# Paged attention of a decoder step: keys turned by VectorE in 32x32 blocks, scores on quarter rows

## The chip, the cores and the metric

The kernel runs on one core of a Trainium2 chip. The metric is the device time of one launch in microseconds (us); the median of several runs counts. One further execution was profiled, and all rows below come from it.

## The reference, cut to what matters

The program is one step of a two-layer decoder for a prompt of 512 tokens and for 8 samples of 8 new tokens each. All of it is float32. The second layer's attention has 8 heads over a shared latent of 512 channels and a rotary key of 64:

```python
def latent_scores(q_lat, q_rope, c, kr):
    s = jnp.einsum('bqhc,bkc->bhqk', q_lat, c, ...)
    s = s + jnp.einsum('bqhr,bkr->bhqk', q_rope, kr, ...)
    return s * SM_SCALE
...
    past_c = cache_kv_latent[page_table].reshape(DB, past_len, KV_LORA)
    past_kr = cache_k_rope[page_table].reshape(DB, past_len, QK_ROPE)
```

Each sample has its own 2048 past keys, in 16 pages of 128 keys that `page_table` names, and its 8 new ones; softmax runs over both, and the probabilities are multiplied with the same latents. For one sample there are 8 heads x 8 tokens = 64 query rows. The pages are 16 x (256 + 32) KB for a sample and 37.7 MB for all eight. The change touches this attention of the samples and the last head of the prompt's attention before it. The convolution, the MLPs and all projections stay.

## The kernel before

Everything is scheduled by hand with semaphores, and each engine works its own list in order. SP (SyncE) issues nearly all loads. PE (TensorE) runs the dense products, about 9,600 matmuls of 128x128 by 288 columns in three parts of float32r (L2422 to L2424). Their weights land in `RAW`, a ring of 4 slabs, and ScalarE (L733) and GpSimd (L1416, L1418) split them into high and low parts `WH` and `WL`.

The prompt's attention goes head by head (L2948 on). For each of four blocks of queries there are scores (`head_scores`, L2908 and L2909, counted by `s_mm`), mask and top on VectorE, the exponential on ScalarE, and the turn of the probabilities (`head_turn`, L2918). Once a head comes its output (`head_out`, L2928, counted by `pv_mm`) and the samples' latent queries (`head_uk`, `head_latent`, kept in `QLAT`). In the last head PE also puts the samples' rotary queries in order (`sample_ropes`, L2936, `QRS`).

The samples' attention follows, as `sequence(i, ...)` for eight samples; 1 to 6 are a loop (`Fori`). A slab is four pages in one place of `RAW`. For each slab j of sample i PE does this, in this order (L3072 to L3087):

- `scores(j, i)`: 5 steps of 128 channels (the last for the rotary part), each for two halves of the slab on separate column tiles: 64 query rows to PSUM partitions 0 to 63 and 64 to 127 of bank 2 (L3025);
- `keys(...)` of the next slab: 16 + 2 transposes of 128x128 (L2983, L2988) into PSUM, which ScalarE (L1323) and VectorE (L2294, L2308) copy to `KEYS` and `ROPES`;
- `values(j - 1, i)`: probabilities times latents, 4 matmuls of 512 columns (L3059), each of them two instructions, as every float32 matmul is;
- `turn(j, i)`: the two transposes of the probabilities (L3035), after VectorE's top (L2315) and ScalarE's exponential (L1340).

Once a sample come the new keys (`new_keys`, L3013 and L3014), the exchange between the two halves (`swap`, L3043) and the output (`give`, L3068). VectorE rescales and adds up the outputs (L2339, L2342). Behind the last slab PE goes on with the output projections (`product("wo", ...)`, and `w_uv` at L3111).

On SP, `cache_loads` is a loop over samples:

```python
            with sp.Fori(0, NS) as i:
                sp.dma_start(table[:], io["page_table"][bass.ds(i, 1), :]).then_inc(table_in, 16)
...
                for j in range(RING):
                    pages = [sp.value_load(table[0:1, 4 * j + q:4 * j + q + 1], min_val=0,
...
                    sp.wait_ge(pe_read_raw, 1 + j + RING * i)
...
                    for q in range(4):
```

In its innermost body there is one DMA for a page's latents (L464, 128 rows of 2 KB) and one for its rotary keys (L468, 128 rows of 256 B). The wait says that PE has read the slab that lay there. A `value_load` (L456) reads one page number into a register. `dense("wo", ...)` (L496) and the two slabs of `w_uv` (L618) are issued behind `cache_loads`.

## Time and profile before

| | us |
|---|---|
| median of 3 runs (1822.06 to 1822.7) | 1822.65 |
| the profiled execution, its own time | 1821.97 |
| its span, in which the rows are counted | 1820.2 |
| PE busy | 1735.6 (95%) |
| VectorE busy | 914.2 (50%) |
| ScalarE busy | 739.2 (41%) |
| GpSimd busy | 966.6 (53%) |
| DMA, mean over the span | 109 GB/s |

A row of a group gives the line, the engine, the operation, the output and inputs with their shapes, the count, the busy time in us and the mean of one in ns, and then the engine's idle time before it with what ended it. Busy time counts stretches in which instructions overlap once, so that 640 matmuls of 384 ns can be busy for 76 us. Register, semaphore and DMA-issuing instructions are not counted as busy; the latter are seen on the timeline of their queue (SPq, ACTq). PEclk is the share of full speed (2.4 GHz) that was granted.

### The profile page before, as it was taken

Reading aid. Unit: us, or ns where it says so; the run is one execution under the profiler, and the core shown is the slowest. Engines: PE = TensorE matmul, PEld = TensorE weight load, DVE = VectorE, ACT = ScalarE, POOL = GpSimd, SP = SyncE. Lnnn points to the kernel's source line nnn. Section 1 sums busy time; section 2 is a strip of 40 time slices with the busy share of each in tenths; the row PEclk is TensorE's granted clock in tenths of the full one; section 3 lists DMA queues with packets and bytes.
Section 4 is the critical chain, followed back from the end, with each engine's and each line's share of the span. In section 5 each row is a group of like instructions: output and inputs, shape, how many; then the busy total and the mean of one; then the engine's idle time right before and its main releaser. Section 6 shows DMA issues by size and latency. Waiting matters only on the chain. (4 is left out here: it accounts for less than half of the span.)

```text
span 1820.2 us, 33590 instructions
## 1 busy us (share of the span) xinstructions
PE 1735.6 (95%) x12402; PEld 1578.6 (87%) x12402; DVE 914.2 (50%) x2228; ACT 739.2 (41%) x1463; POOL 966.6 (53%) x795
## 2 busy tenths in 40 slices
PE   7998899999999999899899899999989999999998
PEld 6997799998899999898776566666989999999988
DVE  5897799943423636673455444444261222222283
ACT  5565444454444543632233333333343222232342
POOL 4994799977799984753210000002655445554652
PEclk9998999999999999999999999999999999999999
DMA  7321455544355540323002155556412222322201
GB/s 205 106 87 56 121 180 163 163 152 139 117 162 162 164 148 26 120 66 117 13 0 79 52 157 156 156 155 207 139 63 77 70 92 92 92 69 69 93 24 53
DMA packets 183947, 198.58 MB, mean 109 GB/s; under 512 B 33065, under 2 KB 138115, under 8 KB 183826
## 3 DMA queue, kind: packets, MB, share of 16 engines
q1 hardware_dynamic: 179726, 194.28, 34.8%
q10 hardware_dynamic: 4100, 2.68, 0.5%
q8 instruction: 76, 1.25, 0.3%
q14 instruction: 45, 0.37, 0.1%
HBM read 192.14 MB, written 4.79 MB: 108 GB/s over the span
## 5 line engine op out<-in xcount | busy, mean ns | idle before, releaser
L1418 POOL TENSOR_TENSOR WL<-RAW,WH 128x1024 fp32r<-128x1024 f32 (+3 forms) x279 | 574.4, 2067 | 256.1 <-ACT WH L733 254.5
L2422 PE MATMUL bank<-AH,WH 128*128 128x288 f32 x2080 | 626.3, 301 | 30.6 <-DVE AL L1672 13.9
L2423 PE MATMUL bank<-AL,WH 128*128 128x288 f32 x2080 | 617.0, 297 | 0.0
L2424 PE MATMUL bank<-AH,WL 128*128 128x288 f32 x2080 | 616.7, 297 | 0.0
L2422 PEld LDWEIGHTS bank<-AH,WH 128*128 128x128 f32 x2080 | 394.6, 190 | 42.2 <-DVE AL L1672 16.7
L733 ACT ACTIVATE WH<-RAW 128x1024 fp32r<-128x1024 f32 (+1 forms) x281 | 292.0, 1045 | 264.9 <-PE bank L2424 264.4
L2423 PEld LDWEIGHTS bank<-AL,WH 128*128 128x128 f32 x2080 | 394.8, 190 | 0.7
L2424 PEld LDWEIGHTS bank<-AH,WL 128*128 128x128 f32 x2080 | 394.5, 190 | 0.0
L2422 PE MATMUL bank<-BH,WH 128*128 128x288 f32 (+1 forms) x1120 | 336.9, 301 | 13.7 <-DVE S L1721 4.1
L1416 POOL TENSOR_TENSOR WL<-RAW,WH 128x256 fp32r<-128x256 f32 (+2 forms) x135 | 119.2, 903 | 416.4 <-ACT WH L733 416.4
L2424 PE MATMUL bank<-BH,WL 128*128 128x288 f32 (+1 forms) x1120 | 333.4, 298 | 0.0
L2423 PE MATMUL bank<-BL,WH 128*128 128x288 f32 (+1 forms) x1120 | 333.3, 298 | 0.0
L2422 PEld LDWEIGHTS bank<-BH,WH 128*128 128x128 f32 x1120 | 210.5, 188 | 19.1 <-issue 15.2
L2424 PEld LDWEIGHTS bank<-BH,WL 128*128 128x128 f32 x1120 | 210.6, 188 | 1.4
L2423 PEld LDWEIGHTS bank<-BL,WH 128*128 128x128 f32 x1120 | 210.6, 188 | 1.3
L1797 DVE SCALAR_TENSOR_TENSOR bank<-S,taps,bank 128x224 f32<-128x224 f32 x464 | 134.7, 365 | 0.0
L1998 DVE TENSOR_TENSOR prod<-R,bank 128x288 f32<-128x288 f32 x64 | 29.0, 454 | 176.3 <-ACT R L1083 100.5
L2007 DVE TENSOR_TENSOR Y<-Y,bank 128x288 f32<-128x288 f32 x112 | 50.7, 453 | 110.9 <-PE bank L2424 110.9
L1443 POOL TENSOR_TENSOR acc<-acc,sq 128x288 f32<-128x288 f32 x97 | 78.5, 815 | 31.6 <-ACT sq L751 26.9
L1591 POOL TENSOR_TENSOR BL<-prod,BH 128x288 fp32r<-128x288 f32 x64 | 51.3, 806 | 67.1 <-ACT BH L1087 67.1
L3025 PE MATMUL bank<-Y,prod 128*64 128x256 f32 x640 | 76.1, 384 | 0.5 <-ACT Y L1323 0.4
L1885 DVE TENSOR_TENSOR Y<-Y,bank 128x288 f32<-128x288 f32 x112 | 49.7, 448 | 49.0 <-PE bank L2424 49.0
(298 smaller groups left out, 2131.6 us busy)
## 6 DMA issues: line engine op xcount, KB each, us to landing
RAW<-in_w_up SPq DMA_DIRECT2D x48, 1024.0 KB, 5.5
RAW<-in_w_down SPq DMA_DIRECT2D x48, 1024.0 KB, 5.1
RAW<-in_cache_kv_latent SPq DMA_DIRECT2D x128, 256.0 KB, 2.9
RAW<-in_conv_pw SPq DMA_DIRECT2D x16, 512.0 KB, 7.3
RAW<-in_conv_pw SPq DMA_DIRECT2D x8, 1024.0 KB, 5.2
RAW<-in_ple_gate SPq DMA_DIRECT2D x8, 1024.0 KB, 5.1
RAW<-in_cache_k_rope SPq DMA_DIRECT2D x128, 32.0 KB, 2.9
RAW<-in_w_o SPq DMA_DIRECT2D x4, 1024.0 KB, 6.1
```

Source lines behind the costliest of these rows:

```text
L733: nc.scalar.activation(split_part(WH, d, q), raw_part(d, q), ACT.Copy).then_inc(hi_done, 1)
L1416: nc.gpsimd.tensor_tensor(dst[:, 0:a], src[:, 0:a], hi[:, 0:a], ALU.subtract)
L1418: nc.gpsimd.tensor_tensor(dst, src, hi, ALU.subtract).then_inc(lo_done, 1)
L1443: nc.gpsimd.tensor_tensor(dst, dst, src, ALU.add).then_inc(acc_done, 1)
L1591: nc.gpsimd.tensor_tensor(half(BL, m, h), prod[:, n % 2, :], half(BH, m, h).bitcast(F32), ALU.subtract).then_inc(u_lo, 1)
L1797: nc.vector.scalar_tensor_tensor(out=run if c < CW - 1 else out, in0=src, scalar=w, in1=run, op0=ALU.mult, op1=ALU.add).then_inc(conv_late, 1)
L1885: nc.vector.tensor_tensor(half(Y, m, h), half(Y, m, h), bank[u % BANKS][:, 0:H], ALU.add)\
L2007: nc.vector.tensor_tensor(half(Y, m, h), half(Y, m, h), bank[u % BANKS][:, 0:H], ALU.add)\
L2422: nc.tensor.matmul(out, wh, xh, start=first, stop=False)
L2423: nc.tensor.matmul(out, wh, xl, start=False, stop=False)
L2424: return nc.tensor.matmul(out, wl, xh, start=False, stop=last)
L3025: ins = nc.tensor.matmul(bank[2][64 * g:64 * g + 64, 0:256], q, k, start=c == 0, stop=c == 4)
```

## The change

A unit is now eight pages (1024 keys), two for a sample, 16 in all; all loops over units on PE, ScalarE and VectorE are written out.

- PE no longer transposes pages. VectorE turns them in 32x32 blocks, from SBUF to SBUF: `turn_pages` 4 pages with 2048 elements a partition in one instruction, `turn_ropes` 256. A page's turned keys lie together in `TURN` (576 columns a page: 18 blocks of 32 channels), so that the write is one run and a matmul reads four runs of 32, one from each of four pages.
- After such a turn the four quarters of the partitions hold different keys, and each has 32 channels at a time. `scores(u)` is 18 blocks x 4 quarters x 2 column halves = 144 matmuls, of 32 rows, 64 columns and 128 moving columns. The quarters write to four banks, the halves to two sets of partitions.
- The queries must lie in each of the quarters. `queries(i)` does that with 18 DMAs of 256 B rows from SBUF to SBUF, issued by ScalarE: for sample 0 ahead of the last exponential of head 7, for the others behind the even units.
- The units lie in `RAW` (two slabs) and in `WIDE`, a place over `WH` and `WL`, in turn. Unit u takes the place of u - 4 and waits for `unit_read`, which `values` counts. The high parts of `wo` wait for 14 units read, the low parts for 15.
- The new keys of all samples are multiplied at once and masked (`KZ`, `NMASK`), with no gather and no transposes for each sample.
- On SP, samples 0 and 1 are issued in pieces, each piece when its room is free, and samples 2 to 7 in a loop of two samples. A number, a latent DMA and a rotary DMA for each page stay.

The core of the diff:

```diff
-        bank = [ctx.enter_context(nc.psum_tensor(f"bank{i}", [P, 512], F32)) for i in range(8)]
+        PS = ctx.enter_context(nc.psum_tensor("bank", [P, 8, 512], F32))
+        bank = [PS[:, i, :] for i in range(8)]
...
-        QRS = S[:, 5184:5696]
+        QRS = [S[:, 5184:5696], R1[:, :, :].rearrange("p a b -> p (a b)")[:, 0:TP]]
+        Q4 = [S[:, 1152 * e:1152 * e + 1152].rearrange("p (b q) -> p b q", b=18) for e in range(2)]
...
+        TURN = [TURNED, yflat.rearrange("p (k c) -> p k c", k=8)]
...
+            pages_of(slice(0, 1))
+            sp.wait_ge(ones_set, 1)
+            sp.wait_ge(lo_done, PART0[DENSE0["kvh"] + 4])
+            sp.wait_ge(pe_read_raw, 2)
+            for s in range(2):
+                pages = [page(4 * s + q) for q in range(4)]
+                load_latents(0, s, pages)
+                load_ropes(0, s, pages)
+            sp.wait_ge(kvt_done, NH)
+            sp.wait_ge(v_mm, NH // 2)
+            for s in range(2):
+                load_latents(1, s, [page(8 + 4 * s + q) for q in range(4)])
+            sp.wait_ge(s_mm, 4 * NH)
+            for s in range(2):
+                load_ropes(1, s, [page(8 + 4 * s + q) for q in range(4)])
+            pages_of(slice(1, 2))
+            for s in range(2):
+                load_latents(2, s, [page(4 * s + q) for q in range(4)])
+            sp.wait_ge(pe_read_raw, 4)
+            sp.wait_ge(pv_mm, NH)
+            for s in range(2):
+                load_ropes(2, s, [page(4 * s + q) for q in range(4)])
+            for s in range(2):
+                pages = [page(8 + 4 * s + q) for q in range(4)]
+                load_latents(3, s, pages)
+                load_ropes(3, s, pages)
+            with sp.Fori(1, NS // 2) as i:
+                for e in range(2):
+                    pages_of(bass.ds(2 * i + e, 1))
+                    for k in (2 * e, 2 * e + 1):
+                        pages = [page(8 * (k % 2) + q) for q in range(8)]
+                        sp.wait_ge(unit_read, 4 * i + k - 3)
+                        sp.wait_ge(ones_set, 1)
+                        for s in range(2):
+                            load_latents(k, s, pages[4 * s:4 * s + 4])
+                            load_ropes(k, s, pages[4 * s:4 * s + 4])
...
+            def queries(i):
+                for m in range(4):
+                    for a in range(4):
+                        act.dma_start(Q4[i % 2][32 * a:32 * a + 32, 0:16].rearrange("p (c m) q -> p m c q", m=4)[:, m],
+                                      QLAT[32 * m:32 * m + 32, :, 64 * i:64 * i + 64]).then_inc(q4_in, 16)
+                for r in range(2):
+                    act.dma_start(Q4[i % 2][:, 16 + r], QRS[r][:, 64 * i:64 * i + 64]).then_inc(q4_in, 16)
...
+                else:
+                    act.wait_ge(ql_used, NH)
+                    act.wait_ge(qrs_c, 2)
+                    queries(0)
...
+            def turn_pages(u, s):
+                dve.wait_ge(*half_landed(u, s))
+                if u >= 2:
+                    dve.wait_ge(score_mm, u - 1)
+                nc.vector.transpose(TURN[u % 2][:, 4 * s:4 * s + 4, 0:CL],
+                                    half_pages(u, s).rearrange("p (k c) -> p k c", k=4)).then_inc(keys_turned, 1)
+            def turn_ropes(u, s):
+                dve.wait_ge(*half_landed(u, s))
+                nc.vector.transpose(TURN[u % 2][:, 4 * s:4 * s + 4, CL:CL + DR],
+                                    half_ropes(u, s).rearrange("p (k c) -> p k c", k=4)).then_inc(keys_turned, 1)
...
+            for u in range(1, UNITS2):
+                i, j = divmod(u, 2)
+                if u < UNITS2 - 1:
+                    turn_pages(u + 1, 0)
+                    turn_pages(u + 1, 1)
+                unit_top(u)
+                if u < UNITS2 - 1:
+                    turn_ropes(u + 1, 0)
+                    turn_ropes(u + 1, 1)
+                unit_sum(u)
+                if j and i:
+                    keep(i - 1)
+                if j:
+                    gain_output(u - 1)
+                else:
+                    finish(i - 1)
+                if j and i < NS - 1:
+                    new_top(i + 1)
...
+            def new_keys(i):
+                pe.wait_ge(q4_in, 16 * Q4_LOADS * (i + 1))
+                if i > 1:
+                    pe.wait_ge(swap_read, i - 1)
+                dst = new_score_bank(i)
+                for c in range(4):
+                    nc.tensor.matmul(dst, QLAT[:, c, 64 * i:64 * i + 64], CS[:, c, :], start=c == 0, stop=False)
+                for r in range(2):
+                    ins = nc.tensor.matmul(dst, Q4[i % 2][:, 16 + r, :], KZ[:, r, :], start=False, stop=r == 1)
+                ins.then_inc(new_mm, 1)
+            def scores(u):
+                pe.wait_ge(keys_turned, CHUNKS * (u + 1))
+                for b in range(18):
+                    for a in range(4):
+                        rows32 = slice(32 * a, 32 * a + 32)
+                        for g in range(2):
+                            ins = nc.tensor.matmul(score_bank(u, a)[64 * g:64 * g + 64], Q4[u // 2 % 2][rows32, b, :],
+                                                   TURN[u % 2][rows32, 4 * g:4 * g + 4, 32 * b:32 * b + 32], start=b == 0, stop=b == 17)
+                ins.then_inc(score_mm, 1)
+            def turn(u):
+                i, j = divmod(u, 2)
+                pe.wait_ge(exp_done, 2 * u + (1 if j else 2))
+                if j == 0 and i > 1:
+                    pe.wait_ge(lat_out, i - 1)
+                for k in range(4):
+                    ins = nc.tensor.transpose(bank[1][:, k * P:(k + 1) * P], SP[:, k * P:(k + 1) * P], ident[:, :])
+                if j == 0:
+                    ins = nc.tensor.transpose(bank[3][0:64, 0:64], PN, ident[0:64, 0:64])
+                ins.then_inc(spt_mm, 1)
...
+            hd = NH - 1
+            head_scores(hd, 0)
+            head_uk(hd)
+            head_turn(hd - 1, 3)
+            head_scores(hd, 1)
+            head_out(hd - 1)
+            head_latent(hd)
+            sample_ropes()
+            head_turn(hd, 0)
+            head_scores(hd, 2)
+            head_turn(hd, 1)
+            head_scores(hd, 3)
+            head_turn(hd, 2)
+            pe.wait_ge(ql_used, NH)
+            pe.wait_ge(qrs_c, 2)
+            new_keys(0)
+            scores(0)
+            head_turn(hd, 3)
+            head_out(hd)
+            pe.wait_ge(pt_used, 4 * NH)
+            for c in range(4):
+                ins = nc.tensor.transpose(bank[6][0:TS, c * P:(c + 1) * P], CS[:, c, :], ident[:, :])
+            ins.then_inc(csn_mm, 1)
+            turn(0)
+            for u in range(1, UNITS2):
+                i, j = divmod(u, 2)
+                if u == 1:
+                    pe.wait_ge(csn_set, 1)
+                    pe.wait_ge(a_lo, A("o", 0, NH - 1))
+                scores(u)
+                if j and i:
+                    give(i - 1)
+                values(u - 1)
+                turn(u)
+                if j and i < NS - 1:
                     new_keys(i + 1)
-            keys(0, 0, range(3))
-            pe.wait_ge(a_lo, A("o", 0, NH - 1))
-            pe.wait_ge(ql_used, NH)
-            keys(0, 0, (3, 4))
-            new_keys(0)
-            sequence(0, True, False)
-            with pe.Fori(1, NS - 1) as i:
-                sequence(i, False, False)
-            sequence(NS - 1, False, True)
-            values(3, NS - 1)
+            values(UNITS2 - 1)
             product("wo", None, 0, 1)
             give(NS - 1)
-            pe.wait_ge(swap_read, NS)
...
```

`values(u)` and `give(i)` do the same matmuls as before, in other places; `unit_top(u)` is one reduction over four banks and two small instructions for eight pages, where `slab` had that for four. `set_constants` takes the place of `set_dup` in head 1, with some eight small instructions more; `sample_ropes` does its eight matmuls twice.

## Rows read from the trace of the kernel before

**Rows 1.** The page, section 4: the chain that ended last, shares of the span.
```profile
PE bank L2422 9%; PE bank L2424 9%; PE bank L2423 9%; PE bank L3025 4%; PE bank L3059 3%; PE bank L2983 3%; PE bank L3035 1%; DVE bank L1700 0%; PE bank L3068 0%; PE bank L3052 0%; PE bank L2988 0%; DVE X L1710 0%; POOL WL L1416 0%; PE bank L3136 0%; PE bank L3013 0%
```

**Rows 2.** 1060 to 1260 us: length; PE, PEld, DVE, ACT, POOL busy; PEclk; DMA share; GB/s.
```profile
1060.00:1260.00 200.00, 200.00 (x1453) 121.00 (x1451) 94.09 (x258) 72.56 (x212) 1.10 (x1) 1.00 0.53 156
```

**Rows 3.** Groups of PE instructions: total busy us, mean ns | idle before.
```profile
L3025 PE MATMUL bank<-Y,prod 128*64 128x256 f32 x640 | 76.1, 384 | 0.5 <-ACT Y L1323 0.4
L2983 PE MATMUL bank<-ident,RAW 128*128 128x128 f32 x512 | 63.0, 277 | 0.0
L3059 PE MATMUL bank<-RAW,S 128*64 128x512 f32 x256 | 61.9, 604 | 0.0
...
L3035 PE MATMUL bank<-ident,scaled 128*128 128x128 f32 x64 | 13.9, 299 | 0.0
L2988 PE MATMUL bank<-ident,RAW 128*128 128x128 f32 x64 | 12.2, 273 | 0.0
```

**Rows 4.** Timeline of PE: start us, duration us, instructions; new keys, last values.
```profile
1054.00 0.63 PE L3013 MATMUL bank<-acc,prod 128*64 128x8 f32 x8
...
1234.04 0.63 PE L3013 MATMUL bank<-acc,prod 128*64 128x8 f32 x8
...
1262.85 1.94 PE L3059 MATMUL bank<-RAW,S 128*64 128x512 f32 x8
```

**Rows 5.** SP's page loads by line: duration ns min/median/max; landing of the latents.
```profile
L464 SPq DMA_DIRECT2D RAW<-in_cache_kv_latent x128: 332/333/360, 969.7 to 1245.0; - x128
...
DMA to landing us min/median/max: 2.4/2.9/3.2
L468 SPq DMA_DIRECT2D RAW<-in_cache_k_rope x128: 332/333/933, 970.3 to 1245.5; - x128
```

**Rows 6.** Timeline of SP: start us, duration us, the DMA issued.
```profile
1155.51 0.33 SPq L468 DMA_DIRECT2D RAW<-in_cache_k_rope  x1
...
1160.90 0.34 SPq L464 DMA_DIRECT2D RAW<-in_cache_kv_latent  x1
...
1164.54 0.33 SPq L468 DMA_DIRECT2D RAW<-in_cache_k_rope  x1
1167.54 0.33 SPq L464 DMA_DIRECT2D RAW<-in_cache_kv_latent  x1
...
1245.53 0.33 SPq L468 DMA_DIRECT2D RAW<-in_cache_k_rope  x1
...
1261.52 3.68 SPq L618 DMA_DIRECT2D RAW<-in_w_uv  x2
```

**Rows 7.** Waits of SP's queue, 900 to 1300 us: total, times, longest.
```profile
SPq L464 <- PE bank L3059: 27.2, 10, 17.9
```

**Rows 8.** Timeline of PE: L3111, two column tiles, all pairs.
```profile
1272.13 3.71 PE L3111 MATMUL bank<-RAW,Y 128*64 128x128 f32 x64
```

**Rows 9.** Groups of VectorE, 1060 to 1260 us: total busy us, mean ns.
```profile
L2342 DVE SCALAR_TENSOR_TENSOR S<-S,acc,bank 128x512 f32<-128x512 f32 x20 | 15.0, 748 | 21.1 <-PE bank L3059 21.1
...
L2283 DVE COPY prod<-S 128x256 f32 x6 | 1.7, 278 | 0.0
```

**Rows 10.** Timeline of PE in the last head: idle before in brackets.
```profile
1008.50 0.33 PE L2918 MATMUL bank<-ident,prod 128*128 128x128 f32 x1 [2.16 <-DVE prod L2231]
...
1013.22 1.02 PE L2909 MATMUL bank<-S 128*128 128x512 f32 x2
```

**Rows 11.** Head outputs on PE's timeline; 1017 to 1023 with the columns of rows 2.
```profile
1003.91 2.42 PE L2928 MATMUL bank<-S,root 128*128 128x512 f32 x8 [0.17 <-ACT S L1287]
...
1018.72 4.63 PE L2928 MATMUL bank<-S,root 128*128 128x512 f32 x8 [0.69 <-ACT S L1287]
...
1017.00:1023.00 6.00, 5.24 (x12) 3.02 (x13) 0.36 (x2) 0.60 (x1) 0.00 (x0) 0.52 0.33 101
```

**Rows 12.** SP's issue of 2 KB rows, beside ScalarE's (L549) and alone (L631).
```profile
L549 SPq DMA_DIRECT2D Y<-in_x_prompt x8: 400/432/615, 0.8 to 4.9; - x8
L631 SPq DMA_DIRECT2D out_y_prompt<-Y x8: 332/356/567, 1805.4 to 1817.1; - x8
```

More of the change, by code:

```diff
@@ L274, in decoder_step @@
             pass
+        with nc.sbuf_tensor("TURNED", [P, 8, 18 * 32], F32) as TURNED:
+            pass
         BH, BL = sb("BH", [P, FC, T], F32R), sb("BL", [P, FC, T], F32R)
@@ new lines, in page, with load_latents @@
+            def page(n):
+                return sp.value_load(table[0:1, n:n + 1], min_val=0, max_val=io["cache_kv_latent"].shape[0] - 1)
+            def load_latents(u, s, pages):
+                dst = half_pages(u, s).rearrange("p (a c) -> p a c", a=1)
+                for q in range(4):
+                    sp.dma_start(dst[:, :, q * CL:(q + 1) * CL],
+                                 io["cache_kv_latent"].rearrange("n p c -> p n c")[:, bass.ds(pages[q], 1)])\
+                        .then_inc(half_landed(u, s)[0], 16)
@@ L2253, in _ @@
+            for hd in range(NH - 1):
                 top(hd, 0)
@@ L2367, in sequence @@
-            def sequence(i, first, last):
-                for j in range(4):
-                    slab(j, i, first, last and j == 3)
-                    if j:
-                        gain_output(j - 1, i)
-                    elif not first:
-                        finish(i - 1)
-                if not last:
-                    new_top(i + 1)
-            nc.vector.memset(QSR, 0.0).then_inc(qsr_zero, 1)
-            nc.vector.memset(NKR[DR:P], 0.0).then_inc(qsr_zero, 1)
-            nc.vector.memset(col(TOP, 4), NEG).then_inc(qsr_zero, 1)
@@ L2940, in _, with give @@
+            def give(i):
+                pe.wait_ge(out_done, OUTS + OUTS * i)
+                if i < NS - 1:
+                    pe.wait_ge(spt_c, 3 * (i + 1) + 2)
+                for c in range(4):
+                    ins = nc.tensor.matmul(give_bank(i)[:, c * 64:(c + 1) * 64], OUT[:, c * P:(c + 1) * P], JOIN,
+                                           start=True, stop=True)
+                ins.then_inc(out_mm, 1)
             rot(1, QR[:, 0, :])
@@ L2947, in _ @@
             pe.wait_ge(kv_staged, 10)
-            for hd in range(NH):
-                more, pair = hd < NH - 1, hd % 2 == 1 and hd < NH - 1
+            for hd in range(NH - 1):
+                pair = hd % 2 == 1
                 head_scores(hd, 0)
@@ L2960, in _ @@
                 head_uk(hd)
-                if not more:
-                    sample_ropes()
                 head_turn(hd, 1)
@@ L3063, in give @@
-            def give(i):
-                pe.wait_ge(out_done, OUTS + OUTS * i)
-                pe.sem_inc(seen, 1)
-                for c in range(4):
-                    ins = nc.tensor.matmul(bank[7][:, c * 64:(c + 1) * 64], OUT[:, c * P:(c + 1) * P], JOIN, start=True,
-                                           stop=True)
-                ins.then_inc(out_mm, 1)
-            def sequence(i, first, last):
-                for j in range(4):
-                    scores(j, i)
-                    if j == 1 and not first:
-                        give(i - 1)
-                    if not (last and j == 3):
-                        keys(*((j + 1, i) if j < 3 else (0, i + 1)), range(5))
-                    if j:
-                        values(j - 1, i)
-                    elif not first:
-                        values(3, i - 1)
-                    turn(j, i)
-                if not last:
-                    new_keys(i + 1)
@@ new lines, in _ @@
+            head_out(hd - 1)
+            head_latent(hd)
+            sample_ropes()
+            head_turn(hd, 0)
[8 more added lines that the diff above has]
+            head_turn(hd, 3)
+            head_out(hd)
+            pe.wait_ge(pt_used, 4 * NH)
+            for c in range(4):
+                ins = nc.tensor.transpose(bank[6][0:TS, c * P:(c + 1) * P], CS[:, c, :], ident[:, :])
```

522 lines of the change are left out of this document (243 added, 279 removed).

## The prediction

> **What bounds the kernel now.** The page's chain that ended last is PE all through, and after the dense products it names three lines of the paged attention: L3025 (scores), L3059 (values) and L2983 (page transposes) [rows 1]. The change touches that stage and the last attention head before it, so I asked for the stage alone: from 1060 to 1260 us PE is busy without a gap, VectorE 94 of 200 us, ScalarE 73, the DMA engines 53% at 156 GB/s [rows 2]. The groups of PE say what it does there: scores 76.1 us, page transposes 63.0 + 12.2, values 61.9, transposes of weights 13.9 [rows 3]. One sample (four slabs of four pages) takes (1234.04 - 1054.00) / 6 = 30.0 us of PE [rows 4]. PE bounds the stage.
>
> Next I asked what comes right behind PE. The page doesn't show it, because DMA-issuing and register instructions are not counted as busy; the timeline of SP, which issues every page load, does. Its DMAs start 0.52 us apart (7 spacings from 1160.90 to 1164.54), and from the last of a slab to the first of the next there are 3.0 us: a spacing, 0.2 for waits, and four page numbers read, 0.55 to 0.57 each [rows 5, 6]. So a sample costs SP 32 x 0.517 = 16.5, 16 x 0.55 = 8.8, the page table with the loop's end 2.5 (the 5.4 us from 1155.51 to 1160.90, less a spacing, four numbers and a wait), four waits 0.8: **28.6 us of SP, against 30.0 of PE**. The waits agree: SP waited 27.2 us for L3059, 17.9 of it at once, so 9.3 / 6 = 1.5 us a sample [rows 7]. SP is 5% away from being the bound.
>
> **What the change takes off PE.** All page transposes, 75.2 us. The scores become 144 matmuls a unit (8 pages), of 32 rows, 64 columns and 128 moving columns. No matmul on quarter rows is in the trace. The nearest is L3111, two column tiles side by side with 128 moving columns: 64 instructions, which are 16 pairs in two passes, in 3.71 us, 0.232 us a pair [rows 8]. If all eight tiles run side by side, a unit's scores cost 18 x 0.232 = 4.2 us; if the four row groups follow one another, four times that, 16.7. I take 4.2: the pair shows that separate tiles overlap, and the row groups write to four different banks. Values and weight transposes keep their work. A sample is then 30.0 - 75.2/8 - 76.1/8 + 2 x 4.2 = 19.5, with the wider new-key matmuls about 20: **10 us of PE a unit, against 15.0**.
>
> The Trainium skill ("TensorEngine Tiling (Array Packing)", Instruction Overhead) has a rule against many small matmuls: each has an overhead of about 60 cycles, however small. By it the 288 instructions of a unit take 7.2 us (an estimate, at 2.4 GHz), and the last scores would end 3 us later than in the sum below. No trace here has such matmuls yet.
>
> **What it adds, and what hides it.** VectorE turns 2048 elements twice a unit and 256 twice. No 32x32 turn is in the trace; the nearest, an SBUF copy of 128x256, took 278 ns, 1.07 ns an element, so 2.2 and 0.3 us (lower end); as an upper end I take four times that, since no row limits it; I take the lower, as passes here go by their elements. With a top over 512 (at most 0.75), its scale, the sum, the gain of 0.75 and half a finish and a keep, a unit costs VectorE 5.1 + 3.4 = 8.5 us [rows 9]. ScalarE loses its key copies and gets 18 DMAs a sample, 6 to 11 us at 0.35 to 0.6 each. The DMA engines get 2304 packets of 256 B a sample more, at 53% now [rows 2]. All of this lies under SP's pace, below; without that cover the units would go at PE's 10.
>
> **What it leaves.** SP's work for a page: one number, one latent DMA, one rope DMA. Only two of four waits and every second loop end go: 28.6 - 0.5 = **28.1 us a sample, 14.05 a unit**. So PE hands the bound to SP, and 8 of the 10 us a sample that PE gains become waiting for `keys_turned`. SP itself waits for no buffer: unit u takes the place of u - 4, which was read about 15 us before.
>
> **The sum**, along SP's queue. It goes on at the prompt's last scores (`s_mm` 32), in the trace at 1013.22 + 1.02 = 1014.2 [rows 10]. Head 7 gets a turn of pages ahead of its first mask (2.2) and a doubled `sample_ropes` (1.9, where PE now waits 2.2, so mostly covered): with the constants of head 1, +3.0, so 1017.2. Then ropes of unit 1 (8 numbers, 8 DMAs: 8.5), the table 2.2, latents of unit 2 (8.5), its ropes (8.5), unit 3 (12.7): 40.4. The wait for `pv_mm` among them comes at 1036.4; the last head's output stands behind queries(0) and scores(0) on PE and should be there at about 1034: nothing, with 2 us to spare. Six samples: 168.6. **SP's last issue is done at 1226.2**; before, it is at 1245.9 [rows 6].
> The tail: landed 2.9 after its start [rows 5], 1228.6; the second half turned 2.2, the top of unit 14, which stands between, 0.9, ropes 0.7: 1232.4; scores 4.2, give 1.1, values(14) 3.8 (two slabs of 1.94, overlapping [rows 4]), turn and copy 1.3, swap and values(15) 4.1: 1246.9.
> PE now idles some 4 us in each unit. Where it waited just before the stage, the granted clock was 0.52 for 6 us, that is mostly at 1.2 GHz, and eight matmuls took 4.63 us that took 2.42 before [rows 11]. Earlier units absorb such a loss; I add 2.2 once, at the end: 1249.1.
> ScalarE issues DMAs at the same time as SP. Where both issued, in the kernel's first 6 us, SP's DMAs of 2 KB rows took 432 ns (median), alone at the end 356 [rows 12]: 0.08 more. Of the 126 from queries(1) on, two thirds meet one of SP's: 0 to 8 us on the queue. I take 4: 1253.1. Before, the last values end at 1264.8 [rows 4]. Gain 11.7.
> Behind it, both slabs of w_uv come free only with values(15), where before the first came free 3.3 us ahead of the second; they were issued at 1261.5 and 1264.8 and used at 1272.1 [rows 6, 8]. About 1.5 us of that shows now. The low parts of wo, held until values(14), need 2 us and have 5: nothing. **Net -10.2 us**: 1821.97 - 10.2 = 1811.8 against the profiled execution's own time (its span is 1820.2, 1.8 less); the median of the runs shown, 1822.65, is 0.7 above it, so **1812**. (Cross-check: 6 x (30.0 - 28.1) = 11.4 in the loop.) About 0.2%, 3.6 us, is what a measurement of this kernel can tell from no change.
>
> **Rivals.**
> A, the forecast: SP's issue is the bound, 1801 to 1818. Chance 0.62.
> B, no change that shows: A, with the ScalarE DMAs at their upper end (+4), scores near 7 us (+3), and `pv_mm` late, since 18 DMAs stand ahead of exp(7,3) on ScalarE (+2): about 1821. 0.13.
> C, slower: issue is one path for both queues, and each of the 126 DMAs holds SP for its own 0.333 us, 42 us in the place of my 4: 1850. It decides from 0.11 us a DMA on (14 us, A's gain and 4). For it: 432 against 356. Against it: that is a quarter of the price. In part or whole 0.09.
> D, slower: an engine's new work is dear. With row groups in series PE needs 16.7 + 5.8 = 22.5 a unit; sixteen from about 1026 end at 1026 + 360 + 4 = 1390, 125 us later: 1947. PE overtakes SP from scores of 14.05 - 5.8 = 8.2 us a unit. Turns at four times the copy's rate give VectorE 5.1 x 4 + 3.4 = 23.8, about the same end. For it: nothing here shows either operation. Against it: the pair's overlap, and passes that go by elements. 0.11.
> E, all of PE's gain shows: 16 x 10 from 1026, and 4, end at 1190: 1748. SP's spacing would have to shrink; of 256 DMAs the shortest took 332 ns and the median 333 [rows 5]. 0.05.
>
> **How the numbers follow.** Faster: A and E, 0.67. Same: B, 0.13. Slower: C and D, 0.20. The range: below, A without contention (4), the clock's 2.2, head 7's 3 and w_uv's 1.5, 1812 - 11 = 1801, leaving out E; above, B and the smaller half of C, to 1835, leaving out D and the rest of C.
>
> **What would show it.** SP's DMAs in the loop 0.52 us apart, 56 us from one pair of samples to the next, and no wait for `unit_read`. PE idle about 4 us a unit ahead of the scores, released by VectorE's turns, and those by DMA landings. Scores 4 us a unit, turns 2.2 us each. The last values ending near 1253. It is wrong if SP waits for PE (then PE or VectorE bounds), if SP's spacing grows while ScalarE issues, or if page loads are issued sooner than 28 us a sample.

## The result, and the profile after

The kernel after takes **1836.53 us** (median of 5 runs, 1833.14 to 1842.3), the kernel before 1822.7 beside it (1822.06 to 1823.71): ratio 1.0075, 95% interval 1.0053 to 1.0097, slower by 13.8 us. The profiled execution of after is itself at 1836.53, its span 1834.7. The forecast of 1812.0 was wrong in sign, and the range (to 1835.0) missed by 1.5 us.

The page of after: busy time by engine, the granted clock in 40 slices, two DMA queues, and the chain that ended last ([rows 1]).

```profile
PE 1694.4 (92%) x15798; PEld 1562.1 (85%) x15798; DVE 930.7 (51%) x2134; ACT 682.3 (37%) x1296; POOL 967.1 (53%) x795
PEclk9998999999999999999999888889999999999999
q1 hardware_dynamic: 179726, 194.28, 34.0%
q8 instruction: 111, 1.82, 0.4%
PE 65%; DVE 9%; POOL 9%; SPq 7%; issue 5%; ACT 3%; DMA 1%; ACTq 1%; POOLq 0%; DVEq 0%
```

SP's queue (7%) is on the chain now. The same stretch as [rows 2]: PE is busy for 159 of 200 us, at a granted clock of 0.85.

```profile
1060.00:1260.00 200.00, 159.39 (x4132) 102.00 (x4118) 101.82 (x167) 23.07 (x70) 0.00 (x0) 0.85 0.62 179
```

PE's groups from 1026 to 1275 us, all 16 units: busy, mean ns, idle before and what ended it ([rows 3]).

```profile
L3089 PE MATMUL bank<-TURNED,S 32*64 32x128 f32 x2304 | 42.8, 297 | 18.8 <-issue 18.8
L3089 PE MATMUL bank<-Y,S 32*64 32x128 f32 x2304 | 41.9, 289 | 22.4 <-issue 18.2 <-DVE Y L2378 4.2
```

The scores are 84.7 us for 16 units, 5.3 each (4.2 forecast, at full clock), so the row groups do run side by side. But 37.0 us of idle time lies inside them, marked "issue": PE waited for no semaphore. I call such a stretch a hole. The timeline of PE shows them in the middle of a unit's 288 matmul instructions:

```profile
1093.47 3.09 PE L3089 MATMUL bank<-TURNED,S 32*64 32x128 f32 x199
1097.73 1.59 PE L3089 MATMUL bank<-TURNED,S 32*64 32x128 f32 x89 [1.16 <-issue]
1099.24 0.38 PE L3111 MATMUL bank<-S,scaled 128*128 128x2 f32 x2
1099.56 3.65 PE L3127 MATMUL bank<-RAW,root 128*64 128x512 f32 x16
...
1103.90 4.07 PE L3089 MATMUL bank<-Y,S 32*64 32x128 f32 x270
1109.76 0.59 PE L3089 MATMUL bank<-Y,S 32*64 32x128 f32 x18 [1.79 <-issue]
```

Queue 8 of the page carries packets of 16 KB with instructions. From 1060 to 1250 us there are 30 of them for 4,007 matmul and 3,993 weight-load records, 267 a packet, so I take a packet for 256 instructions (an estimate). One is in flight from 1095.34 to 1096.47; the hole ends 1.26 us later. All 19 holes end so, 1.0 to 1.6 us behind the end of a packet. A unit's scores are 144 weight loads and matmuls of two passes, 576 instructions, more than two packets.

Two more groups, over the same 16 units, tell how near PE itself is to the bound: the turn of the probabilities (L3100, its idle time and what ended it behind the bar) and half of the values.

```profile
L3100 PE MATMUL bank<-ident,prod 128*128 128x128 f32 x64 | 10.8, 294 | 7.1 <-ACT prod L1437 4.8 <-ACT S L1441 2.2
L3127 PE MATMUL bank<-WIDE,root 128*64 128x512 f32 x128 | 40.9, 725 | 0.0
```

PE waited for turned keys once (4.2 us, at unit 1) and for exponentials 7.1 us in all. The rest of its time is work and holes: it is as near the bound as SP. The DMA view from 1060 to 1250 us, before and then after:

```profile
q8 instruction: 3, 0.05, 0.1%
```
```profile
q8 instruction: 30, 0.49, 1.1%
```

SP's page loads ([rows 5]): a third of a microsecond as a rule, but some take six times that. Its waits from 1000 to 1280 us ([rows 7]) have none for `unit_read`, as forecast, and one for `pv_mm` (L539) that the sum had at nothing.

```profile
L508 SPq DMA_DIRECT2D RAW<-in_cache_kv_latent x64: 332/333/2022, 971.4 to 1244.6; - x64
...
L508 SPq DMA_DIRECT2D WIDE<-in_cache_kv_latent x64: 332/333/1664, 996.5 to 1230.3; - x64
```
```profile
SPq L498 <- DMA table<-in_page_table: 8.8, 7, 1.8
SPq L539 <- PE bank L3056: 4.2, 1, 4.2
```

SP's timeline ([rows 6]): the end of the prologue (all page loads ahead of the loop of six samples), four stretched groups, the last page load. A sample takes (1247.0 - 1064.55) / 6 = 30.4 us, where 28.1 was forecast.

```profile
1064.55 0.29 SPq L496 DMA_DIRECT2D table<-in_page_table  x1
...
1100.91 1.89 SPq L508 DMA_DIRECT2D WIDE<-in_cache_kv_latent  x4
1102.98 3.19 SPq L516 DMA_DIRECT2D S<-in_cache_k_rope  x4
1106.36 3.38 SPq L508 DMA_DIRECT2D WIDE<-in_cache_kv_latent  x4
1109.92 2.35 SPq L516 DMA_DIRECT2D S<-in_cache_k_rope  x4
...
1245.16 1.88 SPq L516 DMA_DIRECT2D RAW<-in_cache_k_rope  x4
```

SP's records of these six samples add up to 182.5 us, which are 167.3 of its own work and 15.2 of DMA issues longer than 0.333 us: 11 of them meet an instruction packet and cost 10.8 us, 31 meet a DMA issue of ScalarE (3.8), 5 neither (0.6). Most of the 11 lie beside a DMA issue of ScalarE too, but the next run has none of these in the loop, and its 14 loads that meet a packet are stretched just as much. In the kernel before one load is stretched, to 933 ns [rows 5], and it too lies beside an instruction packet.

Last, the tail on PE ([rows 4]). The values end at 1278.7 where 1253.1 was forecast:

```profile
1247.52 2.83 PE L3089 MATMUL bank<-TURNED,S 32*64 32x128 f32 x179
1254.26 3.17 PE L3089 MATMUL bank<-TURNED,S 32*64 32x128 f32 x109 [3.91 <-issue]
...
1257.67 3.65 PE L3127 MATMUL bank<-WIDE,root 128*64 128x512 f32 x16
1261.26 0.66 PE L3100 MATMUL bank<-ident,prod 128*128 128x128 f32 x4
1262.02 3.80 PE L3089 MATMUL bank<-Y,S 32*64 32x128 f32 x250
1267.12 0.90 PE L3089 MATMUL bank<-Y,S 32*64 32x128 f32 x38 [1.31 <-issue]
...
1275.07 3.65 PE L3127 MATMUL bank<-RAW,root 128*64 128x512 f32 x16
```

The last keys' turns of 2048 elements end at 1252.8, so that the hole in unit 14's scores, and values and turns behind it, held unit 15. So the 25.6 us are: SP resumes 1.5 earlier than forecast (1015.7), the prologue is 48.8 long in the place of 40.4 (+8.4), the loop 182.5 in the place of 168.6 and 4 of contention (+9.9), the tail 31.6 in the place of 22.9 (+8.7).

### The profile page after: what moved, and what is told of

It reads as the page before. It is cut to its first block, busy times and chain, and to the rows that moved or that the text cites. A ratio compares the mean times of both kernels' runs of the same rounds, so it can differ in the third digit from the quotient of the medians.

```text
span 1834.7 us, 39585 instructions
## 1 busy us (share of the span) xinstructions
PE 1694.4 (92%) x15798; PEld 1562.1 (85%) x15798; DVE 930.7 (51%) x2134; ACT 682.3 (37%) x1296; POOL 967.1 (53%) x795
## 4 chain that ended last, share of the span: by engine, by line
PE 65%; DVE 9%; POOL 9%; SPq 7%; issue 5%; ACT 3%; DMA 1%; ACTq 1%; POOLq 0%; DVEq 0%
PE bank L2550 20%; PE bank L2552 19%; PE bank L2551 19%; POOL WL L1522 4%; SPq L516 2%; SPq L502 2%; SPq L508 2%; PE bank L3089 1%; ACTq L1400 1%; POOL R L1585 1%; POOL root L1585 1%; PE bank L3056 1%; POOL WL L1520 1%; DVE bank L1803 1%; DVE AL L1775 1%
## 5 line engine op out<-in xcount | busy, mean ns | idle before, releaser
L1437 ACT ACTIVATE prod<-bank,S 128x512 f32<-128x512 f32 x16 | 11.0, 687 | 174.3 <-DVE S L2406 87.9
L1988 DVE TENSOR_TENSOR Y<-Y,bank 128x288 f32<-128x288 f32 x112 | 49.8, 449 | 48.8 <-PE bank L2552 48.8
```

Source lines behind the costliest of these rows:

```text
L1988: nc.vector.tensor_tensor(half(Y, m, h), half(Y, m, h), bank[u % BANKS][:, 0:H], ALU.add)\
```

## The experiments

**Theory I**: TensorE's instructions arrive by the DMA engines, 256 at a time; the new scores use them up so fast that PE runs dry, and each packet holds a page load that SP issues meanwhile. **Theory C** (rival C of the prediction): ScalarE's query DMAs share SP's issue. **Theory W**: PE's own work at a lowered clock, or other waits. Each run stands beside the kernel before, at 1822.7 to 1823.5 us.

### Fewer query DMAs

```diff
-                pe.wait_ge(q4_in, 16 * Q4_LOADS * (i + 1))
+                pe.wait_ge(q4_in, 16 * Q4_LOADS * min(i + 1, 2))
-                if j == 0 and i < NS - 1:
+                if j == 0 and i == 0:
...
```

> The changed kernel, with the quarter-row queries laid out for samples 0 and 1 only; samples 2 to 7 use those again, so their scores are not the reference's. 108 of ScalarE's 144 DMAs are gone, nothing else. Theory S (SP's issue sets the pace, and ScalarE's DMAs stretch it): SP's sample falls from 30.4 to 28.1 us for the six of the loop, the last issue comes 14 us sooner, and the time falls by about 14 us, to 1822. Theory P (PE sets the pace by itself, with its holes and its slow clock): SP's DMAs go back to 0.52 us apart but wait for unit_read instead, and the time falls by less than 4 us.

1831.86 us, ratio 1.0043 (1.0026 to 1.006): 4.7 less than after, for 108 DMAs, no 14. The sample stays at 30.2 us. The stretch beside ScalarE's DMAs is gone, that beside packets is 14.2 us, 14 loads: C is a small part. In this trace SP's last load is done no earlier than in after (1249.1 against 1247.0); it is the tail that is shorter, 24.9 us against 31.6. So neither theory's sign came here: no wait for `unit_read`, and no 28.1 us a sample.

### Fixed pages

SP reads no numbers and issues one DMA for four pages; the second run also has the edit above.

```diff
-                for q in range(4):
-                    sp.dma_start(dst[:, :, q * CL:(q + 1) * CL],
+                sp.dma_start(dst, io["cache_kv_latent"].rearrange("n p c -> p n c")[:, n:n + 4])\
...
```

> The changed kernel, with pages 0 to 15 taken for every sample in place of those of the page table: no page numbers are read, and each half unit is one DMA of four latent pages and one of four rotary pages (4 DMAs a unit where there were 16, the same bytes). The attention of the samples is not the reference's. Theory S: SP's cost of a sample falls from 28 to about 4 us, the units go at PE's own pace, 10 us by its work and about 12.3 with the 2.3 us of holes a unit seen now, the last values end near 1029 + 197 + 4 = 1230, and the time is about 1788. Theory P: the time stays within 5 us of 1836.

> Fixed pages and two query sets together. If ScalarE's DMAs hurt only by stretching SP's issue, this is within 3 us of the kernel with fixed pages alone. If they also hold up the transfers or the scores, it is 5 us or more faster than that.

1870.69 us (1.0266, 1.0249 to 1.0283) and 1869.55 (1.0259, 1.0235 to 1.0283): with SP nearly free the kernel is 34 us **slower**, which neither theory had. SP now waits for PE, and the scores' holes are 66 us:

```profile
SPq L497 <- PE bank L3107: 184.5, 12, 16.7
```
```profile
L3069 PE MATMUL bank<-TURNED,S 32*64 32x128 f32 x2304 | 47.6, 319 | 33.6 <-issue 33.6
L3069 PE MATMUL bank<-Y,S 32*64 32x128 f32 x2304 | 43.3, 296 | 36.6 <-issue 32.3 <-DVE Y L2358 4.2
```

This made instruction supply the suspect. The edit changed more than the density of the loads, as one DMA now brings four pages, so that part isn't parted here. That a packet waits behind bulk transfers in the same DMA engines is how I read it; no run shows the queue itself. The query DMAs cost nothing here (1.1 us).

### Half of the blocks

```diff
-                for b in range(18):
+                for b in range(0, 18, 2):
```

> Fixed pages and two query sets, and every second of the 18 blocks of channels left out of the scores: half of their instructions and of their work, so that the scores are not the reference's. Theory I (PE's holes inside the scores are waits for its instructions, 16 KB or 256 of them at a time): with about 370 instead of 660 PE instructions a unit the holes go, from some 2.3 us a unit to under 0.7. PE's own work falls by 2.1 us a unit, so that VectorE (8.9) or the transfers (about 8.5) bound: about 9.5 us a unit, and the time is 40 us under the one with fixed pages and two sets. If the holes have another cause (keys, queries), they stay at 2 us a unit and the gain is no more than 16 x 2.1 = 34 us less what VectorE holds back.

1761.01 us (0.9648, 0.9613 to 0.9684; half of each sum left out): 109 us less than in the run before, where Theory I had 40 and its rival at most 34. Between 1026 and 1305 us the scores' busy time fell by 48 us and their idle time marked "issue" by 61, from 66.7 to 5.6, and both came off in full:

```profile
L3069 PE MATMUL bank<-TURNED,S 32*64 32x128 f32 x1152 | 21.7, 298 | 0.9 <-issue 0.9
L3069 PE MATMUL bank<-Y,S 32*64 32x128 f32 x1152 | 20.8, 285 | 9.0 <-issue 4.7 <-DVE Y L2358 4.2
```

But work and instructions fell together; the next two part them.

### Same column time, fewer instructions

```diff
-                        for g in range(2):
-                            ins = nc.tensor.matmul(score_bank(u, a)[64 * g:64 * g + 64], Q4[u // 2 % 2][rows32, b, :],
-                                                   TURN[u % 2][rows32, 4 * g:4 * g + 4, 32 * b:32 * b + 32], ...)
+                        bq = min(b, 16)
+                        ins = nc.tensor.matmul(score_bank(u, a), Q4[u // 2 % 2][rows32, bq:bq + 2, :]...,
+                                               TURN[u % 2][rows32, 0:4, 32 * b:32 * b + 32], ...)
```

> The kernel after with the scores in matmuls of 128 query columns (two blocks of 64 side by side) against four pages, where there were two of 64 against four pages each: 72 instead of 144 matmuls a unit, each of two passes, for the same column time of TensorE (18 x 128 columns down the array instead of 36 x 128 over twice as many tiles). All else stays, the page loads, the turns and the queries too. What is left out: the sums are over wrong pairs of blocks, so the scores mean nothing. Theory I (the fetching of TensorE's instructions is the new cost: it makes the 37 us of idle time inside the scores and stretches the issue of page loads on SP by 16 us): instruction packets in the stage fall from 40 to about 22, the excess of SP's issue from 16 to about 8 us, the sample period from 30.4 to about 29, the last two units lose most of their 5 us of holes; 1820 to 1826 us. Theory W (TensorE's own work at the lowered clock, or the wait for the landings, is what costs): the same work, so within 3 us of the 1836 of the kernel after.

> As the run before, with 256 moving columns (all eight pages) and every second block: 36 matmuls a unit, a quarter, again for the same column time (9 x 256). What is left out: half of the blocks, and the sums mean nothing. Theory I: packets about 14, excess of SP's issue about 5 us, sample period 28.5 to 28.8, no holes in the scores; 1815 to 1822 us, a few us below the half. Theory W: within 3 us of 1836.

Half: 1826.41 us (1.0019, 1.0009 to 1.003). Quarter: 1822.91 (1.0, 0.9991 to 1.001). They are 0.4 and 0.9 us above the ranges of Theory I. PE's score time is unchanged, the idle time marked "issue" is gone altogether; the quarter's groups, 1026 to 1275 us:

```profile
L3088 PE MATMUL bank<-TURNED,S 32*128 32x256 f32 x576 | 41.5, 447 | 0.0
L3088 PE MATMUL bank<-Y,S 32*128 32x256 f32 x576 | 39.2, 429 | 4.2 <-DVE Y L2378 4.2
L3099 PE MATMUL bank<-ident,prod 128*128 128x128 f32 x64 | 13.2, 341 | 46.2 <-ACT prod L1437 37.3 <-ACT S L1441 8.9
L3126 PE MATMUL bank<-WIDE,root 128*64 128x512 f32 x128 | 32.6, 598 | 0.0
```

W falls: 80.7 us of score work instead of 84.7, and 13.6 us less time. What the holes took has become waiting, 46.2 us where there were 7.1, and the values, which the edit doesn't touch, take 598 ns an instruction and not 725. So with the holes gone PE has slack again, and only then is it SP alone that bounds. The stretch beside packets goes from 10.8 to 8.9 and 5.6 us, the tail from 31.6 to 22.8 and 22.1, where 22.9 was forecast. The loop itself gives less than Theory I had: 30.0 and 29.8 us a sample, where 29 and at most 28.8 were expected, as more of SP's loads meet ScalarE's DMAs (about 6 us in the quarter, 3.8 in after). The granted clock of the stage stays at 0.86, holes or none: so they don't lower it, as I had thought.

### A loop whose instructions stay

```diff
-            for u in range(1, UNITS2):
+            step_of(1)
+            step_of(2)
+            with pe.Fori(0, 3) as m:
+                for u in range(3, 7):
+                    step_of(u, m)
+            step_of(15)
...
```

> The kernel after, its TensorE program for units 3 to 14 written as a loop of three turns over four units (two samples, about 2,600 instructions a turn) instead of straight code; the same instructions in the same order. Before, whose TensorE runs a loop of one sample (about 500), no instruction packet arrives from 1082.7 to 1249.5 us; after, 38 do. Theory R (a loop's instructions stay with the engine and are not fetched again): the packets of turns 2 and 3 go (40 to about 20), the stretch of SP's issue falls by some 6 us and the holes by 20 us: 1826 to 1830 us. Rival: a body of 2,600 is too long to stay, packets and time as in the kernel after (within 3 us of 1836).

> The same loop over the quarter-count scores (sums that mean nothing, as in the run of that name, 1822.9 us), so about 900 instructions a turn. Theory R with room for that many: packets 16 to about 9, SP's stretch by packets (5.6 us) to about 2: 1818 to 1821 us. With no room: 1823 within 2, and 16 packets.

The full body: 1842.19 us (1.0093, 1.0073 to 1.0114), 5.7 more than straight code (the two intervals overlap), with the packets and the holes still there. The quarter body: 1821.81 (0.9991, 0.9982 to 1.0001), 1.1 less than straight. That time is within 1 us of both expectations and decides nothing; the packets do. DMA view from 1060 to 1250 us, the full body, then the quarter:

```profile
q8 instruction: 34, 0.56, 1.2%
```
```profile
q8 instruction: 4, 0.07, 0.1%
```

From 1127.5 to 1257.0 us no packet comes in the quarter's trace, nor from 1082.7 to 1249.5 in the kernel before, whose loop over samples is written so. So a loop of some 900 instructions stays with the engine and one of 2,600 doesn't; where between them the limit lies, no run shows. The quarter in a loop takes 14.7 us less than the kernel after: that is what I can put to Theory I.

### The kernel before, unrolled

```diff
-            with pe.Fori(1, NS - 1) as i:
+            for i in range(1, NS - 1):
```

> The kernel before, its TensorE's loop over six samples written out straight; the same instructions. If straight code costs something by itself: about 12 more instruction packets between 1082 and 1249 us. Theory I (packets stretch SP's issue where they meet it, and empty TensorE's queue where the instructions are short): SP is 1.4 us a sample behind TensorE there and TensorE's matmuls are longer, so most is hidden: +1 to +6 us, 1824 to 1829. Rival: packets cost nothing by themselves, within 1.5 us of before.

1823.89 us (1.0002, 0.9992 to 1.0011), so the rival is right and not the 1 to 6 us of Theory I. The packets rise from 3 to 11 in the DMA view (1060 to 1250 us), PE stays busy for all 190 us at clock 1.00: straight code costs nothing where the instructions are long and SP isn't the bound.

```profile
q8 instruction: 11, 0.18, 0.4%
```

### Cheap page numbers, after and before

```diff
-                return sp.value_load(table[0:1, n:n + 1], min_val=0, max_val=...)
+                return nc.values_load(table[0:1, n:n + 1], ..., skip_runtime_bounds_check_because="...")
```

> The kernel after with SP reading the page numbers without the two instructions that check their bounds (0.55 us each with it, 16 a sample). Theory S (SP's issue sets the pace of the loop, whatever stretches it): each number read costs about 0.25 us less, so 4 us a sample and 24 us over the six samples of the loop, if nothing else is met before: 1812 to 1816 us, and sample period 26.4. Theory P (TensorE with its holes, about 13 to 15 us a unit, is as near a bound as SP): the period falls only to 28 to 29 and waits of SP for the reading of a unit appear; 1822 to 1830 us. Theory M (the landings of pages, over the same 16 DMA engines as all else, set it): no change within 3 us.

1828.64 us (1.0024, 1.0006 to 1.0041; 1821.45 to 1832.87): 8 less, in P's range. The sample is 28.3 us, not 26.4, in good part because 21 loads now meet a packet (19.3 us, almost twice as much), and SP's last load is done 14.5 us earlier but the values end only 4 us earlier: PE with its holes is the bound by then. Even so, SP's waits for `unit_read`, P's sign, come to 0.7 us.

> Control: the kernel before with the page numbers read without the check of their bounds, which takes 4 us a sample off SP's queue. The prediction holds TensorE for the bound there (30.0 us a sample against SP's 28.6): within 2 us of before, or 0 to 3 us faster by the page loads' slack in the first sample. If SP was the bound of before: 8 to 24 us faster.

1823.89 us (1.0004, 0.9994 to 1.0015). SP's waits for PE from 1040 to 1250 us, shorter but more of them:

```profile
SPq L465 <- PE bank L3060: 37.8, 27, 2.6
```

The premise stands: PE, not SP, bounds the kernel before.

### Who issues the queries, and the last head first

The end of the prompt's attention in the kernel after: ScalarE, then PE.

```profile
1014.92 0.58 ACT L1375 ACTIVATE prod<-bank,tiny 128x384 f32<-128x384 f32 x1 [2.13 <-DVE tiny L2325]
...
1015.76 9.78 ACTq L1400 DMA_DIRECT2D S<-S  x15
...
1026.96 0.69 ACT L1375 ACTIVATE scaled<-bank,tiny 128x512 f32<-128x512 f32 x1 [11.09 <-issue]
```
```profile
1028.23 1.08 PE L3077 MATMUL bank<-S 128*64 128x64 f32 x8 [11.39 <-DMA S<-R]
...
1029.67 4.12 PE L3089 MATMUL bank<-TURNED,S 32*64 32x128 f32 x195
...
1037.43 2.42 PE L3056 MATMUL bank<-S,root 128*128 128x512 f32 x8 [0.69 <-ACT S L1386]
```

The queries' 18 DMAs cost ScalarE 11.8 us, 0.65 each, ahead of the last exponential of the head; PE waits for their landing (11.39 us); the head's output is done at 1039.9.

```diff
-                        act.dma_start(Q4[i % 2][32 * a:32 * a + 32, 0:16]...
+                        pool.dma_start(Q4[i % 2][32 * a:32 * a + 32, 0:16]...
```

> The kernel after with the queries' 18 DMAs a sample issued by GpSimd, which idles for 305 us in the stage, instead of ScalarE, where the first 18 stand ahead of the exponentials of the last quarter of the last head (11.8 us). Theory H (the late end of the last head made SP wait 6.7 us before page loads that the sum had as costless): the last head's sum is ready some 6 to 10 us earlier, SP's wait for it goes, prologue ends at about 1058 instead of 1064.6; 1828 to 1831 us. Rival: the first scores, and with them all after, hang on the queries, and GpSimd's DMAs cost 1 us each or more, so that the first scores come 6 us later or more; SP has slack against them of one unit, so 1834 to 1840 us.

1830.77 us (1.0046, 1.0032 to 1.006): 5.8 less, but not where expected. GpSimd issues one in 0.55 us, and SP's wait for `pv_mm` falls from 4.2 to 0.3 us. But SP's last load is done at 1247.4, as in after: its stretch in the loop fell by 5.6 us, and the landings of the page table's rows, which SP waits for, took 6.5 us more. What shrank is the tail (31.6 to 25.0). In the kernel after the last queries on ScalarE do hold the exponential of unit 13 (ScalarE idle for 13.2 us before it, marked "issue"), but that isn't the cause: it is done at 1244.5, PE works on unit 12's values until 1245.5, and its turn follows without a gap. PE was 3.7 us behind this run's at unit 12's scores already (1220.76 against 1217.02), before those queries are issued, and its hole in unit 14's scores is 3.91 us against 1.24. With page numbers read as they were and all 288 instructions, the tail is about 25 us in the three traces that have no query DMAs on ScalarE in the loop (e1, f3, h5), and 31.6 and 30.7 in the two that have them (after, h1); what links the two isn't shown. With the last head ahead of the first scores as well (PE, ScalarE, VectorE):

```diff
-            new_keys(0)
-            scores(0)
             head_turn(hd, 3)
             head_out(hd)
+            new_keys(0)
+            scores(0)
```

> The kernel after with the queries on GpSimd (1830.8 us alone) and the last head ahead of the first scores; numbers read as they were. Theory S+I: SP's wait for the last head goes (it was covered already in the run with GpSimd alone, whose prologue ended at 1063.9), the first scores start 2 to 3 us later, SP's queue unchanged: within 3 us of 1830.8, and a scatter of some 4 us. If the wide scatter of the run of all three (1806 to 1841) comes from this order and not from the cheap numbers, the scatter here is over 15 us.

1831.55 us (1.0069, 1.0045 to 1.0093; 1827.72 to 1838.88). The prologue is 41.3 us, the 40.4 of the sum within 0.9; the time doesn't follow. In the loop of the profiled execution, the fastest of the four, the stretch beside packets was 12.4 us and the landings of the table's rows took 13.2, where after has 10.8 and 8.0.

> The kernel after with three edits together: the page numbers read without the check of their bounds, the queries issued by GpSimd, and the last head of the prompt (its last turn and its output) ahead of the first scores on TensorE, ScalarE and VectorE, so that SP's wait for it in the prologue (4.3 us in the kernel after, 11.7 us in the run with cheap numbers) goes. By parts: prologue ends at about 1052 instead of 1064.6, the loop takes 6 x 24.1 = 145 us of SP's own work and 15 to 20 us of stretch, so SP's last issue is done at 1212 to 1218 instead of 1247; if SP is the bound all through, with a tail of 25: 1800 to 1806 us. Theory P (TensorE with its holes at 13 to 14 us a unit is the next bound): 16 units from about 1034 on are 208 to 224 us: values(15) end at 1256 to 1264 instead of 1278.7, 1814 to 1822 us.

1829.75 us, median of ten runs from 1806.13 to 1841.0; the six fastest of them give a ratio of 0.9989 (0.9956 to 1.0023). So neither the 1800 to 1806 of a bound by SP nor the 1814 to 1822 of Theory P, though P's sign is there: SP waits for `unit_read` five times, 9.8 us in all, and the tail is 36.8 us. The scatter is 35 us; it is 11 us in h5, without the cheap numbers, and 11 us in f1, with them alone, so it comes with neither by itself. That the page loads meet the packets otherwise from run to run is a guess; only one execution is profiled. What sets a good run apart stays open.

### All three costs away

> Three costs taken away at once from the kernel after: a quarter of the matmuls in the scores (sums that mean nothing) in a loop of TensorE that stays with the engine, the queries issued by GpSimd, and the last head ahead of the first scores. If the account is complete, what is left is the sum of the prediction without its 4 us for ScalarE's transfers: prologue ends at 1053 to 1057, six samples at 28.1 to 28.6 us (the landing of the table row took 1.3 us more a sample beside GpSimd's DMAs), SP's last issue is done at 1223 to 1228, values(15) end 22 to 23 us later: 1805 to 1812 us. If something else holds the time, it stays near the 1821.8 us of the looped quarter: above 1816.

1813.44 us (0.9951, 0.9934 to 0.9967; 1810.37 to 1818.34): the expected 1805 to 1812 but for 1.4 us. The prediction's sum without its contention is 1808, 5.4 us less; 3.0 of them are the landings of the table's rows, which cost that much more here than in after. Prologue 42.3, sample 28.9, tail 24.5 us, but these are from the slowest of the four executions (1818.34), whose values end at 1260.0, 10.9 us behind the sum's 1249.1: 2.5 by a later start of the prologue, 1.9 by the prologue, 4.9 by the loop and 1.6 by the tail. So most of the miss is accounted for; the last 2 to 3 us of the median, and more of that execution, are not.

## Why the prediction was wrong

- **PE bounds before, SP right behind**: right (h4; the page loads wait for PE as before).
- **PE's work**: the overlap was right, and so was the price at full clock. Row groups overlap, 5.3 us a unit at clock 0.85, where 4.2 was forecast. A whole run of 270 is 4.07 us (4.3 for 288), 15 ns each, about 36 cycles at 2.4 GHz. But "10 us of PE a unit" became about 12.1 of work (159.4 busy us of 200, at 15.2 a unit), in part by the clock, below. The Trainium skill ("TensorEngine Tiling (Array Packing)", Instruction Overhead) has about 60 cycles of overhead for each; the trace disagrees, for tiles that run side by side.
- **VectorE's turns**: right. 2.31 us for 2,048 elements (2.2 forecast), 0.42 for 256 (0.33). Rival D fell.

```profile
L2372 DVE STREAM_TRANSPOSE TURNED<-RAW x8: 2304/2311/2314, 1001.1 to 1208.3; 128x2048 f32<-128x2048 f32 x8
```

- **"8 of the 10 us a sample that PE gains become waiting for `keys_turned`"**: this failed. SP does bound the loop as forecast (it never waits for `unit_read`), but PE hardly waits: 4.2 us for keys, once, and 7.1 for exponentials. The time went into holes, 37.0 us in 16 units, and into slower work. Where the holes are gone (the quarter) the waiting appears, 2.9 us a unit where "about 4" was forecast, and ahead of the turn, for the exponential, not ahead of the scores.
- The step that failed is **what the scores add to PE**: I counted their time and not their instructions. A unit went from about 240 of PE's records to 640 (counted between 1060 and 1240 us), the program from a loop that stays to straight code, and no rival had the supply. "28.1 us a sample" took SP's issue for a constant, and each packet that a load meets stretches it. By g1, g2 and h2 the supply is worth 14.7 us of the 24.5 that were missed. In the traces 6.0 of them are in SP's loop (182.5 to 176.5 in h2) and 8.3 in the tail (31.6 to 23.3). The tail's part can't be added to what f3 takes off the same tail (6.6).
- **"The wait for `pv_mm`: nothing, with 2 us to spare"** failed, 4.2 us. The step was its input: 18 query DMAs taken at 0.35 to 0.6 us are 0.65, and they stand on ScalarE ahead of exp(7,3), which rival B named and the forecast left out. The rest of the prologue's +8.4 is stretched issue (3.2) and 0.9 of arithmetic.
- **"I take 4" for ScalarE's contention** was right in size: 3.8 us in the loop, 1.1 in the prologue. That e1 comes out 4.7 us faster agrees by luck, since in its trace SP's loop is only 1.4 us shorter.
- **The clock, 2.2 us once**, failed: the stage ran at 0.85 from start to end, holes or none (0.86 in g1), where before it had 1.00. In the kernel after the low stretches fall on work, as the 725 ns of the values show, where g2's 598 ns is near what such a matmul takes at clock 1.00 (604 in the kernel before, [rows 3]); with PE so near the bound that isn't free. What it costs by itself no run shows.

In short, of the 24.5 us: 14.7 for the instructions' supply (from the kernel after to h2). The queries on ScalarE and the place of the last head are 8.4 (h2 to i1), of which the forecast had 4 as contention, so 4.4. The other 5.4 are still there in i1: 3.0 landings of the table's rows, which i1 brings with it, and 2.4 that stay open, within the scatter of its four runs.

## What to carry to other kernels

Count TensorE's instructions, not only their time: small matmuls in straight code can use up a packet's 256 instructions in 1.9 us (270 matmuls with as many weight loads took 4.07), while packets came at least 3.2 us apart here. Then the engine runs dry, and a DMA issue of SP or ScalarE at that moment can be held for a microsecond. A hand-written loop short enough to stay (900 instructions did, 2,600 did not) brings no new packets. A batch of DMA issues costs its queue 0.55 to 0.65 us each, and whoever waits for the engine behind it pays, so look for what stands behind it in that order.

## What the runs showed of the hardware that I had not expected

- Instructions come during the run: 111 packets of 16 KB, 0.9 to 2.2 us each. The Trainium skill, on its page "Trainium Architecture — The Big Picture" (The software stack), has the streams copied to the engines when the program is loaded. That can't be all of it: the trace has 30 packets in 190 us here.
- A DMA issue on SP that meets such a packet takes 0.7 to 2.0 us and not 0.333; relieving SP (f1) almost doubled these meetings, from 11 to 21.
- With page loads issued more densely, four pages a DMA, the holes grew from 37 to 66 us (e2) and the kernel by 34.
- GpSimd's issue of a DMA between two places of SBUF is 0.548 us, ScalarE's 0.624.
